# Mixer: gate and mLSTM products placed among the differential attention's steps, conv written into its result, half of the adaLN sums at the out-projection

## The reference, cut to what matters

```python
proj = h @ w_in                       # 3592 columns: dq dk dv mq mk mv mo mi mf
y_da = diff_attention(rotary(dq), rotary(dk), dv, lam)   # 4 heads, two softmaxes each
qk = silu(causal_depthwise_conv(concat(mq, mk)))         # 4 taps
y_ml = mlstm(qk, mv, mo, mi + b, mf + b)                 # 4 heads, log-sigmoid gates, sigmoid(mo)
x = x + concat(y_da, y_ml) @ w_out
x = x + cross_attention(rms_norm(x), rms_norm(mem))
x = x + hierarchical_moe(rms_norm(x))                    # 32 experts, streamed from HBM
...                                                      # second block, two layers:
mod = silu(c) @ w_ada[l] + b_ada[l]                      # shift, scale, gate
```

## Time and profile before

| | us |
|---|---|
| median of 3 runs | 1871.83 (1871.01 to 1873.21) |
| profiled execution, its own time | 1871.72 |
| span of that execution, first to last instruction | 1870.4 |
| PE busy | 1663.1 |
| DVE busy | 728.5 |

### The profile page before, as it was taken

One profiled execution on the slowest core, in us unless ns is written; L12 is line 12 of the kernel. 1 busy time (PEld: TensorE's weight loads), 2 busy tenths in 40 slices (PEclk: granted clock), 3 DMA queues, 4 the chain that ended last, 5 costly groups with the idle time before them and its releaser, 6 DMA issues.

```text
span 1870.4 us, 15310 instructions
## 1 busy us (share of the span) xinstructions
PE 1663.1 (89%) x5832; PEld 821.4 (44%) x5832; DVE 728.5 (39%) x1521; ACT 471.7 (25%) x971; POOL 312.8 (17%) x312
## 2 busy tenths in 40 slices
PE   6999957799999969898878888899989999998898
PEld 3344435664445433333333333444445544444553
DVE  2335257632234232111101110439955242996622
ACT  2001014300112110010000000546446233644721
POOL 0000000000000002111111110127415011750600
PEclk9999967899999979898888988898999999899999
DMA  8243101431454169999999999600201230030101
GB/s 312 92 178 124 57 0 63 185 135 45 146 184 179 69 262 415 399 407 404 402 401 416 403 411 385 256 0 13 101 23 46 85 107 0 1 113 23 46 1 45
DMA packets 70960, 324.30 MB, mean 173 GB/s; under 512 B 9290, under 2 KB 12626, under 8 KB 58464
## 3 DMA queue, kind: packets, MB, share of 16 engines
q1 hardware_dynamic: 63552, 308.03, 42.4%
q0 software_dynamic: 6016, 10.51, 1.8%
q10 hardware_dynamic: 1312, 4.72, 0.6%
HBM read 318.95 MB, written 12.67 MB: 177 GB/s over the span
## 4 chain that ended last, share of the span: by engine, by line
PE 58%; DVE 19%; DMA 18%; ACT 2%; issue 2%; POOL 1%; SPq 0%; DVEq 0%; ACTq 0%; POOLq 0%
PE bank L185 54%; DMA arena<-in_w 15%; DVE arena L2360 3%; DVE arena L2358 3%; DMA arena<-h_rows,arena 3%; DVE arena L2330 2%; DVE arena L2346 2%; PE bank L1945 1%; PE bank L544 1%; DVE arena L1139 1%; DVE arena L2400 0%; DVE arena L1251 0%; PE bank L628 0%; DMA arena<-in_params 0%; PE bank L828 0%
## 5 line engine op out<-in xcount | busy, mean ns | idle before, releaser
L185 PE MATMUL bank<-arena 128*128 128x512 f32 (+11 forms) x4964 | 1556.5, 556 | 98.1 <-DMA arena<-in_w 51.4
L185 PEld LDWEIGHTS bank<-arena 128*128 128x128 f32 (+2 forms) x4964 | 716.1, 183 | 868.7 <-issue 787.1
L2561 POOL TENSOR_TENSOR arena<-arena 128x512 f32<-128x512 f32 x180 | 201.2, 1118 | 233.5 <-ACT arena L2171 216.0
L1655 POOL TENSOR_TENSOR arena<-arena 128x1 f32<-128x1 f32 (+2 forms) x44 | 32.2, 733 | 730.8 <-DVE arena L1130 523.7
L1605 DVE TENSOR_TENSOR arena<-arena,bank 64x512 f32<-64x512 f32 x32 | 22.1, 691 | 314.9 <-ACT arena L1096 314.9
L2171 ACT ACTIVATE arena<-arena 128x512 f32<-128x512 f32 x180 | 126.0, 717 | 20.5 <-POOL arena L2561 20.4
L1096 ACT ACTIVATE arena<-bank 64x512 f32<-64x512 f32 x32 | 18.9, 591 | 379.9 <-PE bank L185 379.9
L909 ACT COPY arena<-bank 128x512 f32<-128x512 f32 (+2 forms) x110 | 58.8, 538 | 204.3 <-PE bank L185 171.4
L1676 POOL DMA_INDIRECT y_rows<-arena x32 | 32.1, 1004 | 413.9 <-PE bank L828 275.3
L1599 DVE COPY arena<-bank 128x512 f32<-128x512 f32 x32 | 22.2, 692 | 114.7 <-PE bank L828 108.6
L1139 DVE SCALAR_TENSOR_TENSOR arena<-arena 128x512 f32<-128x512 f32 x84 | 63.2, 752 | 3.0
(11 more groups left out here) (261 smaller groups left out, 874.8 us busy)
## 6 DMA issues: line engine op xcount, KB each, us to landing
arena<-in_w SPq DMA_DIRECT2D x96, 2048.0 KB, 36.0
arena<-in_w_in SPq DMA_DIRECT2D x15, 2048.0 KB, 8.0
arena<-in_w_ada SPq DMA_DIRECT2D x12, 2048.0 KB, 8.5
arena<-in_w_out SPq DMA_DIRECT2D x6, 2048.0 KB, 7.9
arena<-in_w_xk SPq DMA_DIRECT2D x2, 2048.0 KB, 10.8
arena<-in_w_xv SPq DMA_DIRECT2D x2, 2048.0 KB, 14.6
arena<-in_w_xq SPq DMA_DIRECT2D x2, 2048.0 KB, 8.6
arena<-in_w_xo SPq DMA_DIRECT2D x2, 2048.0 KB, 8.4
```

The source lines that it names most:

```text
L185: i = pe.e.matmul(o, l, r, start=first and j == 0, stop=last and j == len(pairs) - 1)
L2561: pool.e.tensor_tensor(yc, yc, k.prod[l][n % 4], ALU.add).then_inc(*k.pool.step("sum", l, f, j))
```

## The change

- `mixer_in` keeps `qk`, `v` and the first two `pe_mod`. The swap of group g is issued after product g+1.
- `gates`, the eight `mqk` and the four `mv` products (13 units) are issued inside the attention's ticks, at ticks 0, 2, 5, 8, 11, 13, 16, 19, 22, 24, 27, 30 and 33, after PE's work of that tick. They use banks 4 and 5, and `das` and `dat` are left with four. ACT copies a unit one tick later, DVE convolves it two ticks later, out of two buffers straight into `MQ`/`MK`; the eight silus stand after the attention.
- The gate rows are worked out at ticks 2 to 13 of the attention (`GATE_AT`).
- The four `mo` products go into the mLSTM heads, between `mls` and `mlo`. ACT copies each, and the sigmoid comes in the memory part.
- The memory's squares and its normalisation go into head 3 of the mLSTM.
- The second layer's two `pe_mod` and their four `dve_ada` go into the out-projection.
- `Y` moves out of `HT`'s room into ring slot 1, the gate rows and conv buffers into slot 3; the ring's cycles and `W_IN_END` follow. The gate weights get a buffer of their own.
- ACT does the first squares ahead of silu(c).

```diff
+    k.GW = view(scr + 4224, 8, 8)
     k.macc = view(NFREE - 1344, 1024)
-    k.Y = view(ht_at, 4, 1024)
+    k.Y = k.ring.views[Y_SLOT](4, 1024)
+    rows8 = k.ring.views[GATE_SLOT](8, 512)
+    k.gp = [rows8[0:4, j, :] for j in range(6)]
+    k.mraw = [rows8[:, 6 + j, :] for j in range(2)]
...
+    R.go_on([0, 1, 2, 3, 4, 1, 3, 0, 2, 4, 0])
+    w_in_part(0)
+    sp_ada(k, sp, *MODS[0])
+    w_in_part(1)
+    sp_ada(k, sp, *MODS[1])
+    w_in_part(2)
+    sp.e.dma_start(k.GW, w_in[:, :, W_IN[7][0]:W_IN[7][1]]).then_inc(*k.gw_in.step("gates"))
+    sp_ada(k, sp, *MODS[2])
+    sp_ada(k, sp, *MODS[3])
+    R.ends[Y_SLOT] = [(P, ("yT", 7))]
+    R.ends[GATE_SLOT] = [(P, ("mlo", 3, 1))]
+    for g in range(3, 7):
+        w_in_part(g)
+    R.go_on([2, 4, 0, 3, 2, 4, 0, 3, 1, 0, 3, 0, 3, 2, 4, 3, 1, 0])
...
+    sp_ada(k, sp, *MODS[4])
+    sp_ada(k, sp, *MODS[5])
+    w_xq_part(0)
+    sp_ada(k, sp, *MODS[6])
+    sp_ada(k, sp, *MODS[7])
+    w_xq_part(1)
+    for l, n in GATES:
+        sp_ada(k, sp, l, 2, n)
...
         pe_by_feature(k, pe, ("qk", g), A, w, g % 4, k.HT)
-        b = B.take(pe, V, "swap", g)
-        pe.wait_ge(*A.done("qk", g))
-        product(pe, b, [(k.C("swap"), k.raw[g % 2])]).then_inc(*P.step("swap", g))
+        if g:
+            pe_swap(k, pe, g - 1)
+        if g == 4:
+            pe_mod(k, pe, 0, 0)
+        elif g == 6:
+            pe_mod(k, pe, 0, 1)
...
-    pe_mod(k, pe, 0, 0)
-    for g in range(8):
-        pe.wait_ge(*R.landed(("w_in", 3 + g // 4)))
-        pe_by_feature(k, pe, ("mqk", g), A, R.at(("w_in", 3 + g // 4), 8, 512), g % 4, k.HT)
-    pe_mod(k, pe, 0, 1)
-    pe.wait_ge(*R.landed(("w_in", 5)))
-    for t in range(4):
-        pe_by_token(k, pe, ("mv", t), A if t % 2 else V, R.at(("w_in", 5), 8, 512), t)
-    pe.wait_ge(*R.landed(("w_in", 6)))
-    for t in range(4):
-        pe_by_token(k, pe, ("mo", t), A, R.at(("w_in", 6), 8, 512), t)
-    pe_mod(k, pe, 1, 0)
-    w = R.at(("w_in", 7), 8, 8)
-    b = B.take(pe, V, "gates")
-    pe.wait_ge(*R.landed(("w_in", 7)))
-    for c in range(8):
-        for m in range(2):
-            i = product(pe, b[32 * m:32 * m + 4, :], [(w[:, c, 4 * m:4 * m + 4], k.HT[:, c, :])], c == 0, c == 7)
-    i.then_inc(*P.step("gates"))
-    pe_mod(k, pe, 1, 1)
+        if t == 0:
+            pe_swap(k, pe, 7)
...
+AMONG = {i * 11 // 4: u for i, u in enumerate([("gates", 0)] + [("mqk", g) for g in range(8)] + [("mv", t) for t in range(4)])}
+AMONG_BANKS = (4, 5)
+
+
+def pe_among(k, pe, what, i):
+    P, A, V, R = k.pe, k.act, k.dve, k.ring
+    if what == "gates":
+        b = k.banks.take(pe, V, "gates", among=AMONG_BANKS)
+        pe.wait_ge(*k.gw_in.done("gates"))
+        for c in range(8):
+            for m in range(2):
+                ins = product(pe, b[32 * m:32 * m + 4, :], [(k.GW[:, c, 4 * m:4 * m + 4], k.HT[:, c, :])], c == 0, c == 7)
+        ins.then_inc(*P.step("gates"))
+    elif what == "mqk":
+        pe.wait_ge(*R.landed(("w_in", 3 + i // 4)))
+        pe_by_feature(k, pe, ("mqk", i), A, R.at(("w_in", 3 + i // 4), 8, 512), i % 4, k.HT, AMONG_BANKS)
+    else:
+        pe.wait_ge(*R.landed(("w_in", 5)))
+        pe_by_token(k, pe, ("mv", i), A if i % 2 else V, R.at(("w_in", 5), 8, 512), i, AMONG_BANKS)
 
...
             if phase == 0:
                 for m in range(2):
-                    b = B.take(pe, A, "das", s, m, among=range(6))
+                    b = B.take(pe, A, "das", s, m, among=range(4))
                     product(pe, b[:, 0:nk], [(k.QT[64 * m:64 * m + 64, h, t * 128:(t + 1) * 128],
                                               k.KT[64 * m:64 * m + 64, h, 0:nk])]).then_inc(*P.step("das", s, m))
...
+                pe.wait_ge(*A.done("v", 3))
+                pe.wait_ge(*V.done("v", 2))
                 pe.wait_ge(*A.done("dat", s))
...
+        if tick in AMONG:
+            pe_among(k, pe, *AMONG[tick])
+        if tick == GATE_AT["rows"]:
+            b = B.take(pe, V, "gs", among=AMONG_BANKS)
...
+GATE_AT = {"in": 2, "abs": 3, "softplus": 4, "sum": 6, "max": 8, "exp": 9, "rows": 12, "out": 13}
...
                     b = B.take(pe, V, "mls", h, s)
-                    pe.wait_ge(*A.done("mqk", 7))
+                    pe.wait_ge(*A.done("mqk silu", 4 + h))
                     product(pe, b[:, lo:512], [(k.MK[:, h, lo:lo + 128], k.MQ[:, h, lo:512])]).then_inc(*P.step("mls", h, s))
+                pe.wait_ge(*R.landed(("w_in", 6)))
+                pe_by_token(k, pe, ("mo", h), A, R.at(("w_in", 6), 8, 512), h)
+                pe.wait_ge(*A.done("mv", 3))
+                pe.wait_ge(*V.done("mv", 2))
                 for u in range(2):
                     b = B.take(pe, V, "mlo", h, u)
                     pe.wait_ge(*V.done("mls", h, 3))
...
@@ -878,7 +925,10 @@
             i = pe.e.transpose(b[:, t * 128:(t + 1) * 128], k.Y[:, t, f * 128:(f + 1) * 128], k.ident)
         i.then_inc(*k.pe.step("yT", f))
     pe.wait_ge(*k.dve.done("yT", 7))
-    pe_out(k, pe, "w_out", k.YT)
+    pe_out(k, pe, "w_out", k.YT, [(0, 0), (0, 1), (1, 0), (1, 1)])
+    pe_mod(k, pe, 1, 0, (7,))
+    pe_out(k, pe, "w_out", k.YT, [(2, 0), (2, 1), (3, 0), (3, 1)])
+    pe_mod(k, pe, 1, 1, (7,))
     pe_cross(k, pe)
     pe_router(k, pe)
     pe_expert_rows(k, pe, 0)
...
+            act_among(k, act, *AMONG[tick - 1])
+        g0, g3 = k.gp[2], k.gp[5]
+        if tick == GATE_AT["softplus"]:
+            act.wait_ge(*V.done("abs f"))
+            act.e.activation(g0, g0, ACT.Exp, scale=-1.0).then_inc(*A.step())
+            act.wait_ge(*A.last())
+            act.e.activation(g0, g0, ACT.Ln, bias=1.0).then_inc(*A.step("softplus"))
+        if tick == GATE_AT["exp"]:
+            act.wait_ge(*V.done("g3"))
+            act.e.activation(g3, g3, ACT.Exp, scale=-1.0).then_inc(*A.step("g3"))
+    for g in range(8):
+        x = (k.MQ if g < 4 else k.MK)[:, g % 4, :]
+        act.wait_ge(*V.done("taps", g))
+        act.e.activation(x, x, ACT.Silu).then_inc(*A.step("mqk silu", g))
 
 
...
                     act.e.activation(k.wt[s][:, lo:lo + 128], NBM[:, lo:lo + 128], ACT.Exp,
                                      bias=bias).then_inc(*A.step("wt", h, s))
+                if h == 3:
+                    act_mem_squares(k, act)
+                act.wait_ge(*P.done("mo", h))
+                act.e.copy(k.MO[:, h, :], B.at("mo", h)).then_inc(*A.step("mo", h))
+
...
+        for t in (2 * n, 2 * n + 1):
+            act.wait_ge(*A.done("mo", t))
+            act.e.activation(k.MO[:, t, :], k.MO[:, t, :], ACT.Sigmoid).then_inc(*A.step("mo gate", t))
...
+        if t:
+            act.wait_ge(*A.last())
+        act.e.activation(k.junk0, k.X[:, t, :], ACT.Square, accum_out=k.x_ss[:, t:t + 1]).then_inc(*A.step("sq", "mix", t))
     act.wait_ge(*k.c_in.done("params"))
     act.e.activation(k.CACT, k.P("c"), ACT.Silu).then_inc(*A.step("cact"))
-    for t in range(4):
-        act.wait_ge(*k.x_in[t].done("x"))
-        act.wait_ge(*A.last())
-        act.e.activation(k.junk0, k.X[:, t, :], ACT.Square, accum_out=k.x_ss[:, t:t + 1]).then_inc(*A.step("sq", "mix", t))
...
         dve.e.tensor_tensor((k.QT if g < 4 else k.KT)[:, g % 4, :], raw, tmp, ALU.add).then_inc(*V.step("rot", g))
-        if g % 4 == 3:
-            dve_next_mod(k, dve, g // 4)
+        if g == 1:
+            dve_mods(k, dve, 0)
+        elif g == 2:
+            dve_mods(k, dve, 1)
+        elif g == 3:
+            dve_mod(k, dve, 0, 0)
+            dve_mods(k, dve, 2)
+        elif g == 4:
...
+def dve_mixer_taps(k, dve, g):
+
+    P, V = k.pe, k.dve
+    x, ac = k.mraw[g % 2], (k.MQ if g < 4 else k.MK)[:, g % 4, :]
+    cw, cb = k.P("mconvw"), k.P("mconvb")
+    dve.wait_ge(*k.act.done("mqk", g))
+    dve.e.tensor_scalar(ac, x, cw[:, g * 4 + 3:g * 4 + 4], cb[:, g:g + 1], ALU.mult, ALU.add).then_inc(*V.step())
+    for j in (2, 1, 0):
+        d = 3 - j
+        dve.wait_ge(*V.last())
+        dve.e.scalar_tensor_tensor(out=ac[:, d:512], in0=x[:, 0:512 - d], scalar=cw[:, g * 4 + j:g * 4 + j + 1], in1=ac[:, d:512],
+                                   op0=ALU.mult, op1=ALU.add).then_inc(*(V.step("taps", g) if j == 0 else V.step()))
+
+
...
+            if what == "mqk":
+                dve_mixer_taps(k, dve, i)
+            elif what == "mv" and i % 2 == 0:
+                dve_copy(k, dve, k.MV[:, i, :, 0:128], B.at("mv", i).rearrange("p (h e) -> p h e", h=4), "mv", i)
+        dve_gates(k, dve, tick)
...
                 for u in range(2):
                     d = k.DN[:, (2 * h + u) % 8, :]
                     b3 = B.at("mlo", h, u)[:, 0:258].rearrange("p (t e) -> p t e", t=2)
...
+def dve_mods_between(k, dve, t):
+    if t == 0:
+        dve_mods(k, dve, 5)
+    elif t == 1:
+        dve_mod(k, dve, 1, 0)
+        dve_mods(k, dve, 6)
+    elif t == 2:
+        dve_mods(k, dve, 7)
 
```

More of the change, by code:

```diff
@@ L546, in pe_features, with pe_mod @@
         i.then_inc(*k.pe.step("hT", tag, f))
-def pe_mod(k, pe, l, part):
-    b = k.banks.take(pe, k.dve, "mod", l, part)
```

(18 more changed lines are left out.)

199 lines of the change are left out of this document (91 added, 108 removed).

## The result

The changed kernel takes 1846.21 us (median of 4 runs, 1838.86 to 1847.8) where the kernel before takes 1872.12 (1871.01 to 1873.21): a ratio of 0.985, with an interval of 0.983 to 0.988. It is faster, by 26 us of medians, where 39.5 were forecast; the time lies in the range, near its upper end.

A forecast was written before the change was run, and what follows sets the result against it. PE was taken to bound the kernel, with 40 us of waiting in 110 to fill, and DMA the experts' stage. Memory products 45.7 us earlier, then -1, +5.3 and +1.9, give -39.5 from 1871.7: 1832.2 us, range 1816 to 1847.

The forecast's parts named there:

- Start: Program's start: reordered squares gain 0 to 1.8 us, 0.5 taken, against the earlier `qk` start at 23.2.
- Input stage: `qk`, swaps and `v` 89.4 us, two `pe_mod` 10.6, sum's wait 0.6; swap waits gone; ends at 123.6.
- Attention: Attention with products among its steps: 116.5 us work, 8.9 waits, 1.6 restarts; 127 us, ending at 250.6.
- the four places named: Attention ticks 6/8, 14/16, 20/22, 28/30, no unit between steps: PE waits 1.7 to 2.2 us each, 3.3 at tick 8.
- mLSTM: Attention's end to memory products: 62.9 us, plus 2.5 for clock and 3.0 for normalisation and transposes; 68.4 in all.
- the very chain: After `mo` in three heads: ACT copies `mo`, then `mlb`, DVE makes `nbm`, then `mls`; PE stands 3.7 us.
- Out-projection: `pe_mod` (1,0) adds 5.3 us; (1,1) falls into a wait, slower transposes behind it cost 1.9; +7.2.
- Passed on: From the cross attention on, stages keep their old lengths, 40 us earlier, as loads shift with PE's progress.
- The cheaper case: Clock stays up behind `pe_mod` and mLSTM waits, half the attention's waits covered: 12 us less, 1820, chance 0.13.
- Rival 2: Short matmuls bring the clock down in each of 13 attention turns: 23 us more, 1855, chance 0.08.
- Rivals 3 and 4: DMA-bound experts' stage swallows the gain: 1868, chance 0.04; attention's unit, convolution and step run serially: 1890, chance 0.05.
- The skill's rules: Table-load drain at mLSTM's start (2.8 us more, 1835); clock falls from idle gaps (`pe_mod` 3.6, not 5.3); forecast followed trace instead.

The follow-up runs named there:

- experiment 6: Changed kernel with each swap right behind its own product again and ACT's silu(c) ahead of the squares; 1858.56 us, ratio 0.992 to the kernel before.
- experiment 3: Changed kernel with 8.6 us of useless 512-column matmuls added in attention ticks 6, 14, 20 and 28; 1844.84 us, ratio 0.984 to the kernel before.
- the second profile of the changed kernel: Changed kernel run again, unedited; median 1846.68 us, profiled execution 1842.58 us.
- Experiment 1: Changed kernel with ACT's copy of `mo` h put behind its copy of `mlb` h+1 in mLSTM; 1832.76 us, ratio 0.978 to the kernel before.
- experiment 5: Changed kernel with `mo` among the attention's steps, except `mo` 3 in mLSTM head 0, and ACT's queue in order of use; 1813.75 us, ratio 0.969.
- experiment 4: Changed kernel with seven of eight one-column matmuls left out of each second-layer `pe_mod` at the out-projection; 1837.35 us, ratio 0.981 to the kernel before.
- experiment 2: Changed kernel with all four `mo` also among the attention's steps, 17 units at ticks 0, 2, ... 32; 1823.62 us, ratio 0.973.

## Why the forecast was right in direction and 15 us too low

Point by point, in the order of the sum; 15.4 us lie between 1832.2 and the profiled 1847.63.

- *Start.* I took 0.5 of a range of 0 to 1.8 us. It was 2.8 (20.42 for 23.2). PE's first transpose, which the squares lead to, starts 2.05 us earlier, already outside what I had allowed: the first square now waits for `x` alone. With the order undone (experiment 6) it is back at 11.71. The other 0.75 us is no gain of the order: the 29 transposes behind it took 5.16 us for 5.91, and between 5.09 and 6.23 in the seven profiles with the new order. The first transpose before and after:

```profile
12.07 0.45 PE L544 MATMUL bank<-arena 128*128 128x128 f32 x1 [12.07 <-DVE arena L1130]
```

```profile
10.02 0.45 PE L567 MATMUL bank<-arena 128*128 128x128 f32 x1 [10.02 <-DVE arena L1200]
```

- *Input stage.* Right to 1.9 us. The swap's 7.7 us went whole (experiment 6), and the two `pe_mod` with their waits cost 6.0 and 7.1 instead of the 5.3 and 5.9 that I had; the clock of the stage is 0.95.
- *Attention, the term that was mis-sized.* I allowed 8.9 us of waits, 1.6 for restarts, and no clock. The waits came to 6.5 us, in the four places named, with 3.06 at tick 8 (3.3 forecast) and 0.90 to 1.63 at the others (1.7 to 2.2). The work itself is 118.7 us at full clock (experiment 3: 127.29 less 8.6) where I had 116.5. What is left of the 135.6 us, 10.4, is some 2 of restarts and some 8 of clock; in the second profile of the changed kernel the clock is some 2. These 8 us, not in the sum at all, are what the stage was longer by, and 135.6 us lies outside the 123 to 132 that I had given as a sign of being right. I had rows that priced just this (7.54 against 5.90 behind a wait of 3.54 us), used them for mLSTM, and did not carry them over to the attention's waits; the forecast gives no reason for that. Experiment 3 shows idleness as the cause for the longest of the four, and makes it likely for the others. That the first profile fell behind all four was partly chance.
- *mLSTM.* Waits as forecast: 1.44 (2.3 forecast), 3.48, 3.58 and 3.58 (3.7 three times), by the very chain. The clock cost was the step that failed: I took 2.5 us between bounds of 0 and 4.8. The stretch of 73.2 us ran at 0.88, which is 8.6 us with its restarts (the 4.8 by which it was longer, the 2.5 allowed, and 1.3 of waits that fell short). Experiment 1, which takes the waits away, gave 16.2 us for 10.6 us of waits, so 5.6 of the 8.6 hang on them; the rest is there without them too (54.53 us at 0.94 are 3.3 us of clock).
- *Out-projection.* +9.6 for +7.2. The two `pe_mod` are 7.2 us of work and take the place of 3.4 us of waits (2.59 and 0.82 before, none after), about as I had them (7.2 and 3.6). The term that is off is the clock: 160 instructions took 65.83 us, 3.4 more than at full clock in experiment 5, and the 32 transposes 6.65, 2.4 more than before: 5.8 where I had 3.6 (1.7 in the 5.3, and 1.9). Taking out seven eighths of the matmuls gave 6.0 back (experiment 4).
- *Passed on.* Right. Of 25.5 us at the start of the cross attention 1.4 are lost within it, where I had nothing; from there the shift is kept whole: 24.2 us at the first expert, 24.1 at the end. The DMA engines are full there as before (part 2 of the page of the kernel after, which answers to the earlier trace rows):

```profile
DMA  8321030554443479999999998601201130030101
```

- *The rivals.* The cheaper case had the clock wrong in the same way, and worse. Rival 2 (1855) had the right term, at nearly three times its size (23 us for some 8), and the wrong cause: the clock does fall in turns of the attention, but behind idle PE and in four turns, not behind short matmuls and in thirteen; with a unit in each turn it is 1.00 (experiment 2). Rivals 3 and 4 did not occur.
- *The skill's rules.* In the table loads between attention and mLSTM the next activation followed the load as in the earlier trace rows, and the wait for it came out at 1.44 us, not above my 2.3; no drain shows. On the clock I had set the page against the one row of `pe_mod` and let the row decide for all cases. The Trainium skill (TensorE: Matmul & The Clock Gate, "HAM oscillation — how this bites in real kernels") puts the falls down to idle gaps between bursts, and for the attention and mLSTM experiments 1 to 3 agree with it. For `pe_mod` they leave it open: in experiment 5 the out-projection with both took 62.44 us, the sum of its parts at full clock (128 x 0.43 and twice 3.6), and in the changed kernel 65.83. So the 5.3 us that I read off one row is not the price of a `pe_mod` everywhere.

## What to carry to other kernels

When work is moved under another stage's waits, spread it so that every turn has some: the turns left empty cost their wait and, in some executions, as much again or more in clock. Ahead of each product that waits, read the other engines' queues in the order of use: one copy standing ahead of another, with no dependence between them, cost 13.5 us here, by medians. And price small waits with their clock from rows of the same kernel, wherever PE is otherwise busy.
